# Output projection of two token blocks at a time, by seven block products instead of eight, in a decoder block kernel in float32

## The reference, cut to what matters

```python
mixed = jnp.concatenate([ret, fox], axis=-1).astype(h.dtype)          # (tokens, 1024)
return jnp.einsum('blc,cd->bld', mixed, w_out)                         # w_out: (1024, 1024)
...
h = layer_norm(ALPHA * h + hybrid_mixer(h, w_in[i], b_forget[i], w_out[i]), ln1_g[i], ln1_b[i])
t = h.reshape(b * l, d)
moe = swiglu(t, ws_gate[i], ws_up[i], ws_down[i]) + routed_experts(t, w_router[i], router_bias[i], ...)
```

## Time and profile before

| | before |
|---|---|
| median of 3 runs | 2913.91 us (2911.79 to 2917.86) |
| span of the profiled execution | 2924.8 us |
| TensorE busy | 2840.5 us, 97% |
| VectorE busy | 1712.9 us, 59% |
| GpSimd busy | 1350.4 us, 46% |
| ScalarE busy | 616.3 us, 21% |
| instructions | 40628 |

### The profile page before, as it was taken

The page is one execution under the profiler, slowest core; times in us unless marked ns, Lnnn a source line. Parts: engine busy times, 40 slices in busy tenths (PEclk is TensorE's granted clock), DMA queues, the critical chain, the costliest instruction groups (busy, mean ns, idle before and its releaser), DMA issues.

```text
span 2924.8 us, 40628 instructions
## 1 busy us (share of the span) xinstructions
PE 2840.5 (97%) x14442; PEld 2069.8 (71%) x14442; DVE 1712.9 (59%) x4617; ACT 616.3 (21%) x1269; POOL 1350.4 (46%) x1140
## 2 busy tenths in 40 slices
PE   8999999999999999998999989999999999999997
PEld 4478888888875555554455767878877777777775
DVE  6665656656346767674677534777677773332326
ACT  2221212110025454552110100011111111111114
POOL 3433534447730110101355335677667666555645
PEclk9999999999999999999999999999999999999999
DMA  6500110101121103014435456889989989999986
GB/s 219 184 6 1 31 45 1 30 15 44 30 77 35 63 30 129 28 33 170 173 137 159 131 198 197 270 277 277 271 277 289 291 271 302 305 304 305 317 258 254
DMA packets 192571, 470.49 MB, mean 161 GB/s; under 512 B 27384, under 2 KB 108104, under 8 KB 166632
## 3 DMA queue, kind: packets, MB, share of 16 engines
q1 hardware_dynamic: 145424, 347.63, 33.3%
q0 software_dynamic: 44640, 111.84, 16.5%
q10 hardware_dynamic: 2304, 8.39, 0.7%
HBM read 349.64 MB, written 118.11 MB: 160 GB/s over the span
## 4 chain that ended last, share of the span: by engine, by line
PE 39%; DMA 6%; DVE 3%; POOL 2%; issue 2%; SPq 1%; another core or an unknown queue 0%; ACT 0%; DVEq 0%; POOLq 0%; ACTq 0%
PE ps L3021 18%; PE ps L2796 6%; DMA moe_xg<-t_rows,index 5%; PE ps L2969 4%; PE ps L2940 3%; PE ps L2852 2%; DVE moe_xT L2097 2%; PE ps L2937 2%; POOL moe_xg L2523 1%; PE ps L2862 1%; PE ps L2815 1%; POOL moe_fin L2605 1%; PE ps L2806 0%; DMA base_rows<-moe_yo,index 0%
## 5 line engine op out<-in xcount | busy, mean ns | idle before, releaser
L2523 POOL DMA_INDIRECT moe_xg<-t_rows,index x433 | 428.6, 990 | 174.7 <-issue 139.2
L3021 PEld LDWEIGHTS ps<-moe_xT,moe_wg 128*128 128x128 f32 x2048 | 352.5, 196 | 54.6 <-issue 31.3
L3021 PE MATMUL ps<-moe_xT,moe_wg 128*128 128x192 f32 (+22 forms) x2048 | 380.0, 338 | 9.3 <-DVE moe_hh L1997 5.4
L3021 PE MATMUL ps<-moe_xT,moe_wu 128*128 128x192 f32 (+22 forms) x2048 | 376.3, 337 | 0.0
L3021 PEld LDWEIGHTS ps<-moe_xT,moe_wu 128*128 128x128 f32 x2048 | 354.2, 197 | 4.8
L2544 POOL DMA_INDIRECT base_rows<-moe_yo,index x100 | 231.0, 2310 | 273.2 <-DVE moe_yo L2111 116.8
L2097 DVE STREAM_TRANSPOSE moe_xT<-moe_xg 128x256 f32<-128x256 f32 x433 | 235.1, 610 | 174.2 <-DMA moe_xg<-t_rows,index 155.9
L1296 POOL TENSOR_TENSOR fox_diag<-fox_c,fox_causal 128x128 f32<-128x128 f32 x128 | 55.8, 457 | 450.9 <-DVE fox_mx L1325 446.1
L2660 ACT ACTIVATE moe_sl<-ps 128x256 f32<-128x256 f32 (+19 forms) x144 | 49.6, 345 | 953.9 <-PE ps L3021 736.8
L1997 DVE TENSOR_TENSOR moe_hh<-moe_sl,ps 128x256 f32<-128x256 f32 (+19 forms) x144 | 49.7, 358 | 292.4 <-ACT moe_sl L2660 194.9
L1319 DVE CUSTOM_DVE_ANT_0 hT<-ps,fox_c 128x512 f32<-128x512 f32 (+7 forms) x320 | 166.3, 560 | 63.0 <-PE ps L1581 62.7
(11 more groups left out here) (373 smaller groups left out, 5052.1 us busy)
## 6 DMA issues: line engine op xcount, KB each, us to landing
moe_wg<-in_we_gate SPq DMA_DIRECT2D x64, 1024.0 KB
moe_wu<-in_we_up SPq DMA_DIRECT2D x64, 1024.0 KB
moe_wd<-in_we_down SPq DMA_DIRECT2D x64, 1024.0 KB
fox_c<-ck SPq DMA_DIRECT2D x8, 1032.0 KB, 8.9
emb_xin<-in_x SPq DMA_DIRECT2D x16, 512.0 KB, 3.9
h_rows<-emb_hr SPq DMA_DIRECT2D x16, 512.0 KB, 2.7
ret_w<-in_w_in SPq DMA_DIRECT2D x16, 512.0 KB, 6.6
moe_yt<-h_rows SPq DMA_DIRECT2D x16, 512.0 KB
```

The source lines that it names most:

```text
L2523: pool.indirect_dma_start(out=xg[g % NXG][:, :], out_offset=None, in_=quarters, in_offset=bass.IndirectOffsetOnAxis(ap=route.index4[:, AT4 ...
L3021: ins = pe.matmul(out, w[:, c, f:FF:FC], xT[u][:, c, 0:n], start=(c == 0), stop=(c == DC - 1))
```

## The change

Two blocks of 128 tokens and the two halves of the input columns (retention, attention) are a 2 x 2 arrangement of tokens A; `w_out` in halves of rows and of columns is a 2 x 2 arrangement B. Strassen's scheme (in Winograd's form) makes the four result blocks from seven products instead of eight. Each product is four matmuls of 512 columns.

- Sums of tokens: `out_token_sums(U)`, four adds of 128 x 512 per pair U of blocks, on GpSimd. Sums of weights: `out_weight_sums`, 16 adds of 128 x 512, once, on GpSimd during the last head pair of attention (`SUM_AT`).
- Sums of results: ScalarE copies the first product from its bank (`first_copy`); VectorE makes `second` and `third` from a bank and that copy, and adds four products to the rows in `yt`; GpSimd adds the three copies to the rows (`add_first`, `add_second`, `add_third`). The banks are three, A, B and C. The residual comes scaled by `ALPHA` from the embedding stage.
- All four orders of the first part are written anew, for pairs: `pick` is split into `pick_groups` and `pick_experts`, `scatter` of the even block into two parts of three DMAs. `shared_up(0)` is split around `turn_t(NX - 2)`.
- The blocks are processed in reversed order (the last 128 tokens first); the final stores undo this.
- `fT` has four buffers; the third and fourth lie over `zrow`, so their first loads wait for the clearing stores (`cleared`). Other tiles share memory in the same way; SP's order follows (`stores`, `hidden`, `mixes`, `feathers` for pairs, behind waits for the pair's products and sums). The zeroing of `hh` goes to the end of the loop.

The diff, cut to its core:

```diff
+        wsum = lambda name, at: Area(nc, "moe", (at, at + 8 * kb))(name, [P, RH, BANK])
+        c0 = self.rows - 4 * 2 * TOK - 64
+        q2 = self.small + 3 * kb
+        self.osum = [wsum("osum1", c0), wsum("osum2", q2), wsum("osum4", c0 + 8 * kb)]
+
+
+def out_weight_sums(eng, ahead, part, c):
+
+    w, (t1, t2, t4), made = ahead.wo, ahead.osum, ahead.osum_set
+    b11, b12, b21, b22 = (w[:, k + c, o:o + BANK] for k in (0, RH) for o in (0, BANK))
+    if part == 0:
+        if c == 0:
+            eng.wait_ge(ahead.wo_s[0], 32)
+            eng.wait_ge(ahead.wo_s[1], 32)
+        eng.tensor_tensor(t1[:, c, :], b12, b11, ALU.subtract).then_inc(made, 1)
+    if part == 1:
+        eng.wait_ge(made, c + 1)
+        eng.tensor_tensor(t2[:, c, :], b22, t1[:, c, :], ALU.subtract).then_inc(made, 1)
+    if part == 2:
+        eng.tensor_tensor(b12, b12, b22, ALU.subtract).then_inc(made, 1)
+    if part == 3:
+        eng.wait_ge(made, RH + c + 1)
+        eng.tensor_tensor(t4[:, c, :], b21, t2[:, c, :], ALU.subtract).then_inc(made, 1)
...
+                    pool.tensor_scalar(brow[:, :], brow[:, :], ALPHA, None, ALU.mult).then_inc(brow_set, 1)
+                    pool.wait_ge(brow_set, 1)
                 pool.wait_ge(scaled, i)
                 pool.tensor_tensor(hr[k][:, :], hr[k][:, :], brow[:, :], ALU.add).then_inc(hrow, 1)
 
...
                 if i >= 3:
                     dve.wait_ge(h_out[k], 16 * ((i - 1) // 2))
                 dve.wait_ge(normed, i + 1)
-                dve.tensor_tensor(hr[k][:, :], xn[i % 2][:, :], grow[:, :], ALU.mult).then_inc(scaled, 1)
+                dve.scalar_tensor_tensor(out=hr[k][:, :], in0=xn[i % 2][:, :], scalar=ALPHA, in1=grow[:, :],
+                                         op0=ALU.mult, op1=ALU.mult).then_inc(scaled, 1)
...
+        SUM_AT = {NT - TILES: 3, NT - TILES + 1: 3, NT - TILES + 2: 3, NT - TILES + 3: 3, NT - TILES + 4: 2, NT - TILES + 5: 2}
...
-                                 mixed[P * m:P * (m + 1), RD * h:RD * (h + 1)].rearrange("(g t) d -> t g d", t=QP)
+                                 mixed[P * (NX - 1 - m):P * (NX - m), RD * h:RD * (h + 1)].rearrange("(g t) d -> t g d", t=QP)
...
-            def residual(i):
+            def out_sum_two(U):
+                dve.wait_ge(first_c, U + 1)
+                dve.wait_ge(projected, product_done(U, O_SIXTH))
+                if U >= 1:
+                    dve.wait_ge(added, 3 * (U - 1) + 2)
+                dve.tensor_tensor(second[:, :], ps[:, BANK_B, :], lead1[:, :], ALU.add).then_inc(drained, 1)
+
+            def out_sum_three(U):
+                dve.wait_ge(projected, product_done(U, O_SEVENTH))
+                if U >= 1:
+                    dve.wait_ge(added, 3 * (U - 1) + 3)
+                dve.tensor_tensor(third[:, :], ps[:, BANK_B, :], lead1[:, :], ALU.add).then_inc(drained, 1)
+
+            def out_add(U, which):
+                product, bank, i, half, pre = {
+                    LATE_LEFT: (O_SECOND, BANK_A, 2 * U + 1, LEFT, None),
+                    EARLY_RIGHT: (O_FIFTH, BANK_C, 2 * U, RIGHT, 3),
+                    EARLY_LEFT: (O_FOURTH, BANK_B, 2 * U, LEFT, 1),
+                    LATE_RIGHT: (O_THIRD, BANK_C, 2 * U + 1, RIGHT, 2),
+                }[which]
+                y = yt[i % NYT]
+                if pre is None:
+                    dve.wait_ge(h_in[i % NYT], 16 * (i // NYT + 1))
+                else:
+                    dve.wait_ge(added, 3 * U + pre)
+                dve.wait_ge(projected, product_done(U, product))
+                dve.tensor_tensor(y[:, half], y[:, half], ps[:, bank, :], ALU.add).then_inc(drained, 1)
+
+            def moments_of(i):
                 y, m = yt[i % NYT], mv[i % 2]
-                dve.wait_ge(h_in[i % NYT], 16 * (i // NYT + 1))
-                dve.wait_ge(projected, 2 * i + 2)
-                dve.scalar_tensor_tensor(out=y[:, :], in0=y[:, :], scalar=ALPHA, in1=wide(ps[:, 2 + 2 * (i % 2):4 + 2 * (i % 2), :]),
-                                         op0=ALU.mult, op1=ALU.add).then_inc(summed, 1)
-                dve.wait_ge(summed, i + 1)
+                dve.wait_ge(drained, drains(i // 2, LATE_RIGHT if i % 2 else EARLY_LEFT))
...
-            for w in range(-1, NX - 1):
-                residual(w + 1)
-                if w >= 2:
-                    number(w - 2)
-                scale(w + 1)
-                if w >= 1:
-                    pick(w - 1)
+            for U in range(PU):
+                x, y = 2 * U - 2, 2 * U - 1
+                if U >= 1:
+                    scale(x)
+                    out_add(U - 1, LATE_RIGHT)
+                    moments_of(y)
+                out_sum_two(U)
+                if U >= 1:
+                    scale(y)
+                out_add(U, LATE_LEFT)
+                if U >= 2:
+                    number(y - 2)
+                if U >= 1:
+                    pick_groups(x)
+                out_sum_three(U)
+                if U >= 1:
+                    pick_experts(x)
+                out_add(U, EARLY_RIGHT)
+                if U >= 1:
+                    number(x)
+                    pick_groups(y)
+                out_add(U, EARLY_LEFT)
+                moments_of(2 * U)
+                if U >= 1:
+                    pick_experts(y)
+            scale(NX - 2)
+            out_add(PU - 1, LATE_RIGHT)
+            moments_of(NX - 1)
+            scale(NX - 1)
+            number(NX - 3)
...
             feathers(0)
+            feathers(1)
             hidden(0)
+            hidden(1)
             sp.dma_start(route.sq[:, :], square).then_inc(route.tables, 16)
-            feathers(1)
...
-            hidden(1)
...
+            hidden(2)
+            hidden(3)
+            sp.wait_ge(cleared, 16 + 32 * NK)
+            feathers(2)
+            feathers(3)
...
+            def out_token_sums(U):
+                (a21, a11), (a22, a12) = ([x[(2 * U + r) % 4] for r in range(2)] for x in (mT, fT))
+                s = osums[U % 2]
+                for r in range(2):
+                    pool.wait_ge(mix_in[(2 * U + r) % 4], 16 * (U // 2 + 1))
+                    pool.wait_ge(f_in[(2 * U + r) % 4], 16 * (U // 2 + 1))
+                if U >= 2:
+                    pool.wait_ge(projected, product_done(U - 2, O_THIRD))
+                pool.tensor_tensor(s[:, 0, :, :], a21[:, :, :], a22[:, :, :], ALU.add).then_inc(osums_set, 1)
+                pool.wait_ge(osums_set, 4 * U + 1)
+                pool.tensor_tensor(s[:, 1, :, :], s[:, 0, :, :], a11[:, :, :], ALU.subtract).then_inc(osums_set, 1)
+                pool.tensor_tensor(s[:, 2, :, :], a21[:, :, :], a11[:, :, :], ALU.subtract).then_inc(osums_set, 1)
+                pool.wait_ge(osums_set, 4 * U + 2)
+                pool.tensor_tensor(s[:, 3, :, :], a12[:, :, :], s[:, 1, :, :], ALU.subtract).then_inc(osums_set, 1)
+
+            def add_first(U):
+                y = yt[2 * U % NYT]
+                pool.wait_ge(h_in[2 * U % NYT], 16 * (2 * U // NYT + 1))
+                pool.wait_ge(first_c, U + 1)
+                pool.tensor_tensor(y[:, LEFT], y[:, LEFT], lead1[:, :], ALU.add).then_inc(added, 1)
+
+            def add_second(U):
+                i = 2 * U + 1
+                y = yt[i % NYT]
+                pool.wait_ge(h_in[i % NYT], 16 * (i // NYT + 1))
+                pool.wait_ge(drained, drains(U, SUM_TWO))
+                pool.tensor_tensor(y[:, RIGHT], y[:, RIGHT], second[:, :], ALU.add).then_inc(added, 1)
+
+            def add_third(U):
+                y = yt[2 * U % NYT]
+                pool.wait_ge(drained, drains(U, SUM_THREE))
+                pool.tensor_tensor(y[:, RIGHT], y[:, RIGHT], third[:, :], ALU.add).then_inc(added, 1)
...
+            front, back = range(TOPK // 2), range(TOPK // 2, TOPK)
+            out_token_sums(0)
+            for U in range(PU):
+                x, y = 2 * U - 2, 2 * U - 1
+                if U >= 1:
+                    norm(x)
+                if U >= 2:
+                    scatter(x - 2, back)
+                add_first(U)
+                if U >= 1:
+                    norm(y)
+                add_second(U)
+                if U >= 2:
+                    scatter(y - 2)
+                add_third(U)
+                if U + 1 < PU:
+                    out_token_sums(U + 1)
+                else:
+                    pool.wait_ge(added, 3 * PU)
+                    pool.memset(hh[0][:, :, :], 0.0).then_inc(hh_set, 1)
+                    pool.wait_ge(projected, product_done(PU - 1, O_SIXTH))
+                    pool.memset(hh[1][:, :, :], 0.0).then_inc(hh_set, 1)
+                if U >= 1:
+                    scatter(x, front)
+            norm(NX - 2)
+            scatter(NX - 4, back)
+            norm(NX - 1)
...
+            def first_copy(U):
+                act.wait_ge(projected, product_done(U, O_FIRST))
+                if U >= 1:
+                    act.wait_ge(drained, drains(U - 1, SUM_THREE))
+                    act.wait_ge(added, 3 * (U - 1) + 1)
```

(72 more changed lines are left out.)

170 lines of the change are left out of this document (98 added, 72 removed).

## The result

The changed kernel takes 2965.31 us (median of 4 runs, 2964.12 to 2978.41) against 2915.89 us (4 runs, 2911.79 to 2922.85) of the kernel before on the same chip: a ratio of 1.0185, 95% interval 1.0158 to 1.0212. It is slower by 54 us by the ratio, and by 49 us by the medians; 2961 us had been forecast.

The account below looks back on a forecast made before the run. TensorE, busy in 97% of 2924.8 us, was taken as the bound. The projection's 262.7 us became 305.9; with the tail and without pair 2's 1.3, 47.5 more on the 2913.91 median gave 2961 us, range 2930 to 2977.

Parts of the forecast that it names:

- What is removed: TensorE in the projection: seven products per pair instead of eight, 3.47 us less a pair, at most 27.8 us over eight.
- The order on VectorE: VectorE from rank(x) to the next turn_t: a 13.0 us chain against 6.9 of cover, stopping TensorE 6.4 us a pair.
- GpSimd beside it: GpSimd's token sums beside VectorE's chain: they hold its short two-SBUF-operand instructions, 1.3 us a pair, bounds 0 to 3.8.
- The second path: GpSimd's scatters, add_third and EARLY_RIGHT, counted from turn_t(x): ends at 22.1 us against rank(x) at 22.6, so barely hides.
- The clock: TensorE behind the stop in each pair: a lower granted clock costs 2.3 us more, bounds 1.6 to 2.9.
- Start and end: Pair 0's sixth product waits behind GpSimd's constants until 1372.2, making pair 0 39.4 us; waits at the end add 5.6.
- The tail: The projection's end: a 2.9 us stop, 1.7 for the clock and 1.0 ahead of shared_up(1), 5.6 us together.
- The sum: Projection from 262.7 to 305.9 us; with the tail 48.8 more, 47.5 after leaving out pair 2's 1.3.
- Rival (a): Same VectorE chain, but the clock stays up or GpSimd holds nobody: 2939 us, or 2947 to 2953; chance 0.22.
- Rival (b): TensorE stays dense at 29.5 us in each pair, only the start costing: 2899 us, 15.2 less; chance 0.11.
- Rival (c): GpSimd's work alone bounds the pair at 30 to 31 us, VectorE keeping up: 2911 us, no change; chance 0.05.
- Rival (d): GpSimd's path passes rank(x) by 2 to 3 us more, the pair taking 42: 2975 us; chance 0.10.

Follow-up runs that it names:

- e2: The changed kernel with VectorE's choice of experts for block y moved behind the next pair's scaling of x and last-half addition; ratio 1.0101 to the kernel before.
- e6: The changed kernel with the same instructions in another order on TensorE, VectorE and GpSimd; ratio 1.0024 to the kernel before.
- e7: The changed kernel with e6's order on three engines and e5's early token sums of pair 0; 2911.07 us, ratio 0.9998 to the kernel before.
- e5: The changed kernel with GpSimd's token sums of pair 0 put ahead of its three waits for constants; ratio 1.0183 to the kernel before.
- e8: e7 with GpSimd waiting for its third addition before the first token sum, second sum before third, third before fourth; ratio 1.0001 to the kernel before.

## Why the prediction was right

Taken by its own steps:

- **What is removed.** 27.8 us as the most that seven products give: pair 1 took 29.56 us against 33.0 for two blocks, so the size is right (29.5 had been put).
- **The order on VectorE**, the step that was to decide, did. The chain went as told, rank to number to groups to add to moments to experts to scale, against the 6.99 us of cover that it starts with (6.9 had been put). Undone in part it gave back 3.4 us a pair (e2); undone altogether, with TensorE's and GpSimd's orders set anew too and the clock's share in it, 47 us of the 54 (e6).
- **GpSimd beside it** was mis-sized: 1.3 us a pair put, inside 0 to 3.8, and 2.4 measured in the three instructions, 2.3 when they were let go. Of the five instructions with two SBUF operands that I had counted two were held, for 0.84 and 1.07 us, not 0.63 each; and the entry copy, which has one such operand and was left out of the sum, was held for 0.50. The second path, add_third and the right-half addition behind it, ended 0.2 us before rank(x) was there (VectorE idle for 0.20), and hid, as said.
- **The clock**: 2.3 put (1.6 to 2.9), 2.5 measured, and shown by filling the stop.
- **One pair** is then 29.8 us of work (TensorE's busy time at full clock in e6 and e7), 8.53 of standing still and 2.5 for the clock, against 29.5, 6.4 + 1.3 and 2.3.
- **Start and end**: pair 0 40.3 (39.4 put), its sixth product at 1372.80 (1372.2 put) behind the constants. The tail is 4.2 (5.6 put), and only in part as told: the wait of 0.96 ahead of shared_up(1) is there, but the stop ahead of the last block's transposes is 0.97 and leaves the granted clock at 1.00, where 2.9 and 1.7 for the clock had been put for it; and ahead of shared_up(0) stands a gap of 1.54 us that I had not foreseen and for which the profile names no releaser.
- **The sum**: pairs 3 to 7 at 40.9 instead of 39.5 are 6.9 us, pair 0 0.9; 41.9 put for the stage becomes 49.7, and the tail 1.4 less. 47.5 was forecast; 53.9 is what the stage and the ratio show, and 49.4 the medians.

Rival (a) falls twice, by the clock and by the held instructions. Rival (b) needed the chain under 6.9 us, and it is 15.5. Rival (c) falls by e2: the pair shrank with GpSimd's work unchanged. Rival (d) didn't come: GpSimd's path stayed ahead.

The Trainium skill (SBUF — State Buffer, Who interferes with whom) says that a VectorE instruction with at most one SBUF input does not contend with GpSimd as long as it is outside the 2-port perf modes, and that `copy`, `cast` and `tensor_scalar` can enter these modes, given the right operands, and then contend. The trace agrees with both halves. The additions with one operand in PSUM kept their 0.69 us beside GpSimd's. The instructions with one SBUF tensor as input that were held are of just the three named kinds: the 128x6 copy (0.67 to 0.91 us, else 0.17), the 128x6 gate instruction, a TENSOR_SCALAR (1.07 to 2.38, else 0.23), and, in pair 1 of the changed kernel, a 128x8 cast (0.87, else 0.17). No run shows in which mode an instruction ran.

## What to carry to other kernels

When work per block is regrouped into pairs, the sum of an engine's work says little; write down the longest chain in program order between what TensorE gives out and what it needs next, and count how much TensorE work lies beside it. Here 15.5 us stood against 7.0, and reordering the same instructions on three engines was worth 47. Removing one wait is only worth what the next one in line leaves over: that decided e5 and e8, where an engine that came early met a queue that had not moved.

## What the runs showed of the hardware

- A short VectorE instruction can be held beyond the GpSimd instruction that it met: 2.83 us for a count addition of 0.23, and 2.38 for a gate of 0.23, through two GpSimd additions of which the second did not wait for the first. Where it was made to wait (e8), the gate took 1.15 us. But in the changed kernel the count addition got in at the end of the one sum that it met (1.07 us), though the next sum did not wait for that one either, so the rule for it is open.
- It works the other way round too. In the changed kernel GpSimd's one-column addition (L2618, at 1551.34) took 1.32 us beside VectorE's 1024-column instruction with two SBUF tensors as inputs, where it takes 0.23 in e5 at 1391.14. In e8 the issue of an indirect DMA (L2637, at 1521.87) took 1.98 us beside such an instruction, against 0.98 at 1518.42 without one.
- A stop of 8.5 us filled with products that nobody reads keeps the full clock: the product behind it takes 3.6 us instead of 5.2.
